# Linear attention's heads: another order for the next head's preparation steps

## The reference, cut to what matters

```python
def step(s, inp):                       # one chunk of 64 tokens
    qc, kc, vc, gc = inp
    cum = jnp.cumsum(gc, axis=2)        # gc: log-sigmoid gates / 16
    last = cum[:, :, -1:, :]
    s_new = exp(last)[..., None] * s + einsum('bhjd,bhje->bhde', kc * exp(last - cum), vc)
    ...
    o = einsum('bhid,bhde->bhie', qc * exp(cum), s) + einsum('bhij,bhje->bhie', scores, vc)
...
y_lat = _gla_readout(ol_f + flip(ol_b), rl, norm_g, w_out)   # RMS norm over a head, times silu(r), @ w_out
```

## Time and profile before

| | us |
|---|---|
| median of 3 runs (lowest, highest) | 2516.99 (2516.23, 2519.70) |
| the profiled execution's own time | 2517.74 |
| its span, first to last instruction | 2516.0 |
| PE busy in the span | 2267.9 (90%) |
| DVE busy | 1588.7 (63%) |
| ACT busy | 1076.0 (43%) |
| heads' stage, first transposes to the last matmul of stream 3 (lines 2639 to 502) | 1925.2 to 2089.5 |
| mean granted clock of TensorE, share of full speed | 0.967 |

### The profile page before, as it was taken

How to read it: one execution, slowest core, us unless ns; L and a number is a source line. 1 busy time by engine, 2 the same in 40 slices (tenths; PEclk the granted TensorE clock), 3 DMA queues, 4 the chain that set the end, 5 groups by cost and what they waited for, 6 DMA issues and landing times. The chain is left out here.

```text
span 2516.0 us, 31937 instructions
## 1 busy us (share of the span) xinstructions
PE 2267.9 (90%) x11349; PEld 1812.1 (72%) x11349; DVE 1588.7 (63%) x2284; ACT 1076.0 (43%) x1628; POOL 123.4 (5%) x201
## 2 busy tenths in 40 slices
PE   4998689899999989877889999999999888799995
PEld 3776566678888877666667888787877676588884
DVE  6655656565557665665665555774543774699996
ACT  3343234443343225342343333413333443588884
POOL 0001110000000000110000000000000000011112
PEclk9999899999999999999999999999999999799997
DMA  7650000222225355200012223354634001699996
GB/s 292 210 184 12 1 34 1 76 84 92 94 79 204 128 166 201 77 1 1 35 43 82 94 92 103 137 172 168 218 109 147 22 1 44 265 410 411 412 412 226
DMA packets 95433, 348.32 MB, mean 138 GB/s; under 512 B 12360, under 2 KB 14520, under 8 KB 95056
## 3 DMA queue, kind: packets, MB, share of 16 engines
q1 hardware_dynamic: 88688, 323.67, 36.1%
q0 software_dynamic: 3888, 14.16, 1.5%
q10 hardware_dynamic: 2736, 8.92, 0.9%
HBM read 333.55 MB, written 21.54 MB: 141 GB/s over the span
## 5 line engine op out<-in xcount | busy, mean ns | idle before, releaser
L500 PE MATMUL ps<-a_hi,w_hi 128*128 128x512 f32 x1344 | 545.1, 406 | 28.5 <-DVE h_lo L406 17.8
L502 PE MATMUL ps<-a_hi,w_lo 128*128 128x512 f32 x1344 | 537.2, 400 | 0.0
L501 PE MATMUL ps<-h_lo,w_hi 128*128 128x512 f32 x1280 | 507.8, 397 | 0.0
L464 DVE TENSOR_TENSOR w_lo<-ring,w_hi 128x1024 fp32r<-128x1024 f32 x178 | 218.1, 1226 | 376.1 <-ACT w_hi L459 375.6
L459 ACT ACTIVATE w_hi<-ring 128x1024 fp32r<-128x1024 f32 x178 | 187.9, 1058 | 510.4 <-PE ps L502 505.0
L500 PEld LDWEIGHTS ps<-a_hi,w_hi 128*128 128x128 f32 x1344 | 255.3, 190 | 98.3 <-issue 26.4
L502 PEld LDWEIGHTS ps<-a_hi,w_lo 128*128 128x128 f32 x1344 | 255.4, 190 | 63.0
L501 PEld LDWEIGHTS ps<-h_lo,w_hi 128*128 128x128 f32 x1280 | 243.1, 190 | 60.8 <-issue 2.9
L3392 DVE TENSOR_TENSOR moe_w_lo<-p,moe_w_hi 128x1024 fp32r<-128x1024 f32 x204 | 240.2, 1219 | 17.8 <-ACT moe_w_hi L3489 12.0
L3489 ACT ACTIVATE moe_w_hi<-p 128x1024 fp32r<-128x1024 f32 x204 | 216.2, 1062 | 68.2 <-PE ps L3432 50.6
L2139 PE MATMUL ps<-p_lo,down_hi 128*128 128x512 f32 x352 | 137.8, 392 | 0.0
(11 more groups left out here) (645 smaller groups left out, 4196.0 us busy)
## 6 DMA issues: line engine op xcount, KB each, us to landing
ring<-in_ffn_up SPq DMA_DIRECT2D x88, 512.0 KB, 3.4
ring<-in_w_in SPq DMA_DIRECT2D x72, 512.0 KB, 5.2
p<-in_moe_gate SPq DMA_DIRECT2D x68, 512.0 KB, 7.1
p<-in_moe_up SPq DMA_DIRECT2D x68, 512.0 KB, 6.8
p<-in_moe_down SPq DMA_DIRECT2D x68, 512.0 KB, 8.4
vt<-in_ada SPq DMA_DIRECT2D x64, 512.0 KB, 4.0
p<-in_ada SPq DMA_DIRECT2D x48, 512.0 KB, 5.5
down_raw<-in_ffn_down SPq DMA_DIRECT2D x32, 704.0 KB, 5.2
```

The lines of the kernel that those rows point to most:

```text
L464: self.c.nc.vector.tensor_tensor(self.c.w_lo[:, s % 2, :], self.c.slot(s), self.c.w_hi[:, s % 2, :].bitcast(F32), ALU.subtract).then_inc(s ...
L500: nc.tensor.matmul(bank, c.w_hi[:, s % 2, at], hi(kt), start=(kt == self.order[0]), stop=False)
L501: nc.tensor.matmul(bank, c.w_hi[:, s % 2, at], lo(kt), start=False, stop=False)
L502: return nc.tensor.matmul(bank, c.w_lo[:, s % 2, at], hi(kt), start=False, stop=(kt == self.order[-1]))
```

## The change

Only the plan of the first three heads changes, so the order in which the same pieces are issued on PE, ACT and DVE:

```diff
     for h in range(GLA_H - 1):
-        steps = alternate(scan["steps"], prep["steps"])
+        steps = [0] * 1 + [1 - i for i in alternate(prep["steps"], scan["steps"] - 1)]
         at = steps.index(0) + 1
         plan += steps[:at] + [2] + steps[at:]
```

## The result

The changed kernel takes 2556.36 us (median of 4 runs, 2555.19 to 2564.62); beside it the kernel before has 2518.31 (4 runs). The ratio is 1.0153, 95% interval 1.0141 to 1.0165: slower by 38 us, where 28 were forecast. The time lies 0.4 us above the stated range; the sign was right and the size was not. Executions in the chip's slower state are left out of every ratio; there is one, of e7 (3573.8 us).

What follows compares the result with a forecast made beforehand. PE's work sets a floor, its in-order waits add about 7 us a head, and any growth is paid in full. Waits of 24.4 us plus 3.5 for the clock, taken as 28 onto the median, gave 2545 us, range 2538 to 2552.

Steps and rivals of the forecast that it cites:

- Place A: Inside each head, PE's wait for the first fold behind DVE's cumulative sums: 7.1 us instead of 3.67, 3.4 more.
- Place B: Late in each head, DVE's scaling now stands between two folds: PE waits 2.0 us where it waited nothing.
- Place C: Head boundary, last outputs to S1, six copies ahead of squares: 13.3 us, 3.5 more; net 2.0, 2.0 and 3.5.
- The sum at full clock: All added waits in the heads' stage at the clock as it was, including 0.7 us in head 0: 24.4 us.
- The clock: Half clock at head boundaries slows means and the third S1: up to 7 us, half taken, 3.5 us.
- rival 1: Clock falls at every boundary and stays low longer, slowing PE's work up to S1: 2552 to 2560 us; chance 0.19.
- Rival 2: Waits inside the heads overlap or are partly given back, so the change costs less: 2530 to 2537 us; chance 0.13.
- Rival 3: All preparation hides under the scan, 2.4 us a head gained: faster, 2510 us; chance 0.05.
- Rival 4: The three growths and the filled waits cancel within 5 us; chance 0.03.

Runs made afterwards that it cites:

- e7: Kernel before, first two preparation steps each one scan step earlier in the first three heads; 2519.2 us, ratio 0.9991 to before.
- e5: Kernel before with sixteen extra matmuls, results unread, in PE's 3.67 us wait behind the cumulative sums; 2525.4 us, ratio 1.0018 to before.
- e4: Changed kernel plus extra unread matmuls, ten ahead of each mean and thirteen ahead of the last head's S1; median 2559.4 us (2541.4 to 2571.3), ratio 1.0161 to before.
- e2: Kernel before with only DVE's scaling step moved between the late folds and the step ahead of it two scan steps earlier; ratio 1.0046 to before.
- e12: The same kernel as e4, run once more; 2567.1 us (2564.8 to 2568.3), ratio 1.0190 to before.
- e6: e4's kernel with 22 more extra matmuls in PE's 7.1 us wait behind the cumulative sums; 2565.3 us, ratio 1.0168 to before.
- e10: Changed kernel with extra matmuls as in e4, but five ahead of each mean and seven ahead of the last S1; 2557.2 us, ratio 1.0151 to before.
- e8: e7's kernel with eleven extra matmuls in its shortened wait for the cumulative sums; 2520.6 us, ratio 1.0001 to before.
- e1: Kernel before with only the last preparation step, with its six ACT copies, moved ahead of the squares; ratio 1.0088 to before.

## Why the prediction was right in its waits and wrong in its sum

**What bounds the kernel, and that no work is added:** right. The stage carries the whole difference, and with equal instructions.

**Place A:** right. Predicted 7.1 us instead of 3.67; measured 7.11, 7.10 and 7.11. The half clock behind it, taken as nothing, costs little since DVE sets the pace: 0 to 1.3 us a head in the profiles of before, e5 and e7.

**Place B:** the wait was right (2.0 predicted; 1.80 three times). Its price was not: the text names no clock at B at all, and at head 0's boundary the clock fell there (the last outputs took 1.97 us; 1.10 at the other two).

**Place C:** the chain was right. Predicted 13.3 us at full clock, and 15.0 with the mean at half; measured 14.8, 14.9 and, in head 0's boundary, 16.2, where the first transposes ran at half too and one DVE operation of S16 took 0.8 us longer. At full clock, in e4, it is 13.2 three times. The copies' wait became 1.03 (1.0 predicted), the squares' 2.37 (2.6), P0's for M's copy 0.74 to 0.79 (0.7).

**The sum at full clock, 24.4 us:** e4, whose clock is full at all three boundaries, has 27.8; the heads with no fall there besides that at A grow by 7.6 and 7.2 (7.4 predicted), and the 3.4 us left lie in head 0, where P0 (2.90) and S1 (5.80 after, 5.74 in e4) run at half clock since P0 was pulled into a stretch that has it.

**The clock:** this is the step that failed. The prediction reckoned with at most 7 us, "the mean's four matmuls", 1.7 for each boundary, and "up to 2 more" for the third S1, and then: "I take half of these 7 us: 3.5". Measured is 38.0 - 24.4 = 13.6: 10.3 that e4 gets back from the first S1 on, and 3.4 in head 0, which the text didn't consider. Of the 10.3 about 0.8 is no clock but the DVE operation of S16 at head 0's boundary. Two things were wrong. First, the price was halved, where the mean was slow at every boundary: the three means took 1.8, 1.6 and 1.7 us more and the third S1 1.6, together 6.8 of the 7 us that the text had before it halved them. Second, about as much again was not priced at all: the 3.4 us in head 0, B's fall at head 0's boundary (some 1.3), and a second fall at the second boundary, ahead of head 2's S1 (5.47 instead of 3.84 us), behind waits of 0.79 and 0.82 us and after 6.5 us of which PE had worked three quarters. So the full price alone would have given 2548, and still not 2556.

What the text has for a fall that may not come, that over a single wait of 1.75 us the clock had stayed at 1.00, doesn't carry: in e2 it fell in one of 2.22 us, and in B's of 1.80 it fell in the changed kernel's head 0 but not in heads 1 and 2, and in e12 but not in e4, the same kernel.

The Trainium skill ("TensorE: Matmul & The Clock Gate", HAM oscillation) tells of a kernel in which every group of matmuls starts at the low clock, since the wait for the next transfer, some 3 to 5 us, is longer than the group's own work of about 2 us. At A the trace agrees: the clock stood at 0.50 behind each of the three waits of 7.1 us. The waits at B and ahead of the mean, 1.80 to 2.37 us, are shorter than those that the page tells of, and the clock fell in them too, but not in every execution: in e4's it was full at all three boundaries.

**The rivals:** rival 1 names the measured time (2552 to 2560), but not how it came: the clock didn't stay low through S0, M and P0. At two boundaries S0's scores took 1.15 us, at head 0's 1.98 with M at full clock behind them; it came back, and at two boundaries it fell again. Rival 2 is excluded by A's wait and by e4; its own sum, 3 x (2 to 3) + 7.5, ends at 2534 and not at 2537. Rival 3, all under the scan, fails where the text put its test: DVE's P5 does not fit between the folds. Rival 4 needed A and B near zero, and they are 7.1 and 1.8 us. The range was too narrow above, since the clock, the largest unknown, had been given no more than 7 us in the forecast's own case.

**What stays open:** why the clock falls in one execution's wait of 1.80 us and not in another's. That the filling is what kept the clock up rests on the one fast profile of e4, on e6's last boundary and on the three full-clock fillings ahead of head 3's S1 (e4, e6, e12), beside the changed kernel's and e10's falls in the same places.

## What to carry to other kernels

Where one list fixes the order on several engines, cost a move by the distance from the instruction that starts a chain to the first one that waits for its end, less the work that the waiting engine still has between them; the waits of this case at A, at B and ahead of the mean came out within 0.3 us. Then ask of each new wait on TensorE, however short, which matmuls stand behind it on the path that sets the end, and price them at half clock in the forecast itself, not as a fraction: here the clock was a third of the loss, and it made 20 us between two executions of one kernel. A step on the way from one head's result to the next head's start (here Ln and Exp, which masks wait behind) must not have copies queued ahead of it that nobody needs yet.

## What the runs showed of the hardware that was not expected

- Steady work didn't keep the clock up in e6, nor bring it back soon. In head 1 it was at 1.00 in the wait of 1.99 us ahead of the filling, at 0.71 over the next 2 us, and then stood at half for 9 us of unbroken work, nearly all of it matmuls of 64 columns; it was full two to four microseconds after each of the three fillings ended. In e5, with no wait ahead of the sixteen, it stayed full. Windows of e6:

```profile
2013.00:2022.00 9.00, 9.00 (x41) 8.82 (x42) 8.72 (x13) 0.00 (x0) 0.00 (x0) 0.50 0.01 2
2024.00:2030.00 6.00, 6.00 (x43) 5.64 (x41) 3.12 (x8) 3.17 (x6) 0.00 (x0) 1.00 0.00 0
```

- A fall that is taken away in one place can come in another, dearer one: in e5 two of three heads got 3.4 to 3.7 us longer although a wait had been filled, and with a filled wait in e8 head 1 got 2.9 us longer than in e7, with its mean at 3.78 us.
- GpSimd's two scalings of the queries (line 2783) took 2.49 to 2.56 us after instead of 2.04, where they run beside DVE's S16. Nothing waited for them, but in head 0's boundary one DVE operation of S16 (line 2919) took 1.48 us beside them instead of 0.69. In e1's head 0 that operation took 1.57 and the two scalings 2.04. That such pairs slow each other is a guess from these rows; no run tested it.
